# Two transformer blocks on one core: fewer key columns for the first token tile, and GpSimd scales the probabilities

## The reference, cut to what matters

```python
# sliding ("swa" in the kernel): chunks of 64 keys, this one and the two before it
mask = (k // 64 <= q // 64) & (k // 64 >= q // 64 - 2)
# forgetting ("fox"): blocks of 128 queries, keys up to the end of the block
s = jnp.einsum('bqhd,bkhd->bhqk', q[:, lo:hi], k[:, :hi]).astype(jnp.float32) * ATTN_SCALE
bias = cum[:, :, lo:hi, None] - cum[:, :, None, :hi]
s = jnp.where(causal, s + bias, NEG)
p = jax.nn.softmax(s, axis=-1).astype(v.dtype)
outs.append(jnp.einsum('bhqk,bkhd->bqhd', p, v[:, :hi]))
```

## Time and profile before

| | before |
|---|---|
| median of three runs | 2392.72 us (2390.62 to 2398.5) |
| span of the profiled execution | 2324.9 us |
| median less that span | 67.8 us |
| TensorE matmuls | 2118.6 us busy, 91% of the span |
| VectorE, ScalarE, GpSimd | 68%, 46%, 22% busy |
| DMA | 683 MB, mean 294 GB/s |

### The profile page before, as it was taken

The page is one execution under the profiler, slowest core; times in us unless marked ns, Lnnn a source line. Parts: engine busy times, 40 slices in busy tenths (PEclk is TensorE's granted clock), DMA queues, the critical chain, the costliest instruction groups (busy, mean ns, idle before and its releaser), DMA issues. The chain is left out here.

```text
span 2324.9 us, 27319 instructions
## 1 busy us (share of the span) xinstructions
PE 2118.6 (91%) x9328; PEld 1530.3 (66%) x9328; DVE 1575.4 (68%) x2602; ACT 1059.4 (46%) x1528; POOL 512.0 (22%) x550
## 2 busy tenths in 40 slices
PE   7999999877777777789999999999999999999996
PEld 6998867322222222247599887578888888888785
DVE  5775237666666666544555432578898998889986
ACT  3495014222222212113444324367777777777764
POOL 0000007777777777720000010000000000000000
PEclk9999999999999999999999999999999999999998
DMA  8544429999999999996254643279999999999993
GB/s 312 172 146 181 168 93 379 404 410 409 410 409 409 409 409 409 409 349 202 91 175 143 228 162 127 100 246 329 362 351 365 350 366 369 344 365 350 367 365 112
DMA packets 356584, 683.39 MB, mean 294 GB/s; under 512 B 14016, under 2 KB 222016, under 8 KB 356352
## 3 DMA queue, kind: packets, MB, share of 16 engines
q1 hardware_dynamic: 279008, 401.24, 50.8%
q0 software_dynamic: 77472, 280.80, 30.5%
HBM read 679.88 MB, written 2.10 MB: 293 GB/s over the span
## 5 line engine op out<-in xcount | busy, mean ns | idle before, releaser
L2264 DVE TENSOR_TENSOR weights_low<-weight_ring,piece_hi 128x2048 fp32r<-128x2048 f32 (+1 forms) x286 | 590.1, 2109 | 42.0 <-ACT piece_hi L1205 36.7
L1465 PE MATMUL psum<-weight_ring,region 128*128 128x512 f32 x988 | 478.2, 610 | 143.0 <-DMA weight_ring<-in_peer_v,region 141.5
L1205 ACT ACTIVATE piece_hi<-weight_ring 128x2048 fp32r<-128x2048 f32 (+1 forms) x286 | 494.7, 1768 | 30.4 <-PE psum L1694 27.8
L1465 PEld LDWEIGHTS psum<-weight_ring,region 128*128 128x128 f32 x988 | 169.2, 189 | 451.6 <-issue 303.0
L2083 DVE CUSTOM_DVE_ANT_0 weight_ring<-weight_ring,psum 128x1024 f32<-128x1024 f32 x224 | 273.6, 1222 | 206.8 <-DMA weight_ring<-in_peer_u,region 206.8
L1681 PE MATMUL psum<-piece_hi,tokens_hi 128*128 128x512 f32 x704 | 284.1, 404 | 2.4 <-DVE work_tok L2316 1.3
L841 POOL DMA_INDIRECT weight_ring<-in_peer_u,region x256 | 247.9, 968 | 140.7 <-DVE region L2057 53.0
L1683 PE MATMUL psum<-piece_hi,tokens_low 128*128 128x512 f32 x704 | 278.1, 395 | 0.0
L1682 PE MATMUL psum<-weights_low,tokens_hi 128*128 128x512 f32 x704 | 277.9, 395 | 0.0
L852 POOL DMA_INDIRECT weight_ring<-in_peer_v,region x256 | 242.3, 947 | 90.7 <-issue 70.3
L1053 ACT ACTIVATE region<-constants,region 128x128 f32<-128x128 f32 x247 | 88.4, 395 | 284.9 <-PE psum L1465 210.8
(11 more groups left out here) (317 smaller groups left out, 3428.7 us busy)
## 6 DMA issues: line engine op xcount, KB each, us to landing
weight_ring<-in_w_exp_in SPq DMA_DIRECT2D x176, 1024.0 KB, 11.8
weight_ring<-in_w_exp_out SPq DMA_DIRECT2D x48, 1536.0 KB, 10.0
weight_ring<-in_w_in SPq DMA_DIRECT2D x12, 2048.0 KB, 7.7
weight_ring<-in_w_ffn_in SPq DMA_DIRECT2D x22, 1024.0 KB, 7.7
weight_ring<-in_w_exp_out SPq DMA_DIRECT2D x8, 2048.0 KB, 8.6
weight_ring<-in_w_out SPq DMA_DIRECT2D x6, 2048.0 KB, 8.4
weight_ring<-in_w_in_fox SPq DMA_DIRECT2D x5, 2048.0 KB, 7.8
weight_ring<-in_w_ffn_out SPq DMA_DIRECT2D x6, 1536.0 KB, 6.6
```

The source lines that it names most:

```text
L1205: act.activation(dst, src, ACT.Copy).then_inc(e_hi, 1)
L1465: ins = pe.matmul(psum[:, peer_bank(t, half), :], diag[:, k, :], v_row(n)[:, 512 * half:512 * half + 512], start=(s < TILES and k == 0), s ...
L2264: dve.tensor_tensor(low_of(n), piece(n), hi_of(n).bitcast(F32), ALU.subtract).then_inc(e_low, 1)
```

## The change

1. For sliding and forgetting heads, tile 0 works on 128 keys (`keys_seen`): its score matmul, the maximum, the exponential and the scaling have 128 columns in place of 256. The transpose of block (key tile 1, token tile 0) is left out, so that three transposes are left and the copy out of PSUM has 384 columns. The second value matmul runs over the last 128 tokens alone. The sink of tile 0 stands in column 128.
2. In all 42 heads GpSimd scales both tiles' probabilities, one instruction for each tile, and counts both on one semaphore. ScalarE's L930 and VectorE's L1844 go, and TensorE waits for that one semaphore.
3. GpSimd's queue: the scalings of each stage are put between its DMAs. Of the norm rows, rows 4 and 5 come ahead of the scalings of att2[0], and the others behind them.

```diff
+CAUSAL = ("swa", "fox")
+def keys_seen(kind, t):
+    return (t + 1) * P if kind in CAUSAL else S
...
+    def turned_blocks(kind):
+        return [(k, t) for k in range(TILES) for t in range(TILES) if k * P < keys_seen(kind, t)]
+
+    def turned_keys(g, k):
+        blocks = turned_blocks(heads[g][0])
+        own_blocks = [i for i, (kk, _) in enumerate(blocks) if kk == k]
+        flat = pt_buf[g % 2].rearrange("p k s -> p (k s)")
+        return blocks[own_blocks[0]][1] * P, flat[:, own_blocks[0] * P:(own_blocks[-1] + 1) * P]
...
+        def probabilities(base, n):
+            for g in range(base, base + n):
+                b = g % 2
+                pool.wait_ge(sums_ready, g + 1)
+                for t in range(TILES):
+                    p = p_buf[b][:, t, 0:keys_seen(heads[g][0], t)]
+                    pool.tensor_scalar(p, p, den[:, 2 * b + t:2 * b + t + 1], None, ALU.mult).then_inc(probs_ready, 1)
+
         pool.wait_ge(product_ready, pl.nth["in", N_IN - 1])
         pool.dma_start(x_tok[:, :, :], a["x"][0].rearrange("(t p) n -> p t n", p=P)).then_inc(x_again, 16)
+        probabilities(pl.att1, N1)
         pool.wait_ge(merged, KD)
...
-        for i in range(4, late_row):
+        ROWS_AHEAD = 6
+        for i in range(4, ROWS_AHEAD):
+            load_row(i)
+        probabilities(pl.att2[0], SH + MH2)
+        for i in range(ROWS_AHEAD, late_row):
             load_row(i)
         pool.wait_ge(cum_ready, 1)
...
+        probabilities(pl.att2[1], SH + MH2)
         pool.wait_ge(normed, HALVES * TILES * 7)
...
-                    copy_out(("T", g), pt_buf[g % 2])
-                if 1 <= i <= n:
-                    g = base + i - 1
-                    b = g % 2
-                    act.wait_ge(sums_ready, g + 1)
-                    for t in range(TILES - 1):
-                        ins = act.activation(p_buf[b][:, t, 0:S], p_buf[b][:, t, 0:S], ACT.Copy, scale=den[:, 2 * b + t:2 * b + t + 1])
-                    ins.then_inc(probs_ready, 1)
+                    flat = pt_buf[g % 2].rearrange("p k s -> p (k s)")
+                    copy_out(("T", g), flat[:, 0:P * len(turned_blocks(heads[g][0]))])
...
-                    n_exp = S + 1 if kind in ("self1", "swa") else S
+                        n_exp = keys_seen(kind, t) + (kind in ("self1", "swa"))
...
+                seen = keys_seen(kind, t)
+                ins = pe.matmul(bank[:, t * S:t * S + seen], queries(kind, h)[:, t * P:(t + 1) * P], keys(kind, h)[:, 0:seen],
+                                start=True, stop=True)
...
-                    pe.wait_ge(probs_ready, g + 1)
-                    pe.wait_ge(last_probs_ready, g + 1)
+                    pe.wait_ge(probs_ready, TILES * (g + 1))
                     bank = begin(("T", g))
-                    for k in range(TILES):
-                        for t in range(TILES):
-                            ins = pe.transpose(bank[:, k * S + t * P:k * S + (t + 1) * P], p_buf[g % 2][:, t, k * P:(k + 1) * P], ident)
+                    for i_turned, (k, t) in enumerate(turned_blocks(heads[g][0])):
+                        ins = pe.transpose(bank[:, i_turned * P:(i_turned + 1) * P], p_buf[g % 2][:, t, k * P:(k + 1) * P], ident)
...
-                        ins = pe.matmul(bank[:, 0:S], values(*heads[g], k), pt_buf[g % 2][:, k, :], start=(k == 0), stop=(k == TILES - 1))
+                        first, turned = turned_keys(g, k)
+                        ins = pe.matmul(bank[:, first:S], values(*heads[g], k), turned, start=(k == 0), stop=(k == TILES - 1),
+                                        skip_group_check=True)
...
-            last = TILES - 1
-            dve.tensor_scalar(p_buf[b][:, last, 0:S], p_buf[b][:, last, 0:S], den[:, 2 * b + last:2 * b + last + 1], None, ALU.mult)\
-               .then_inc(last_probs_ready, 1)
...
-                        dve.tensor_copy(s_buf[b][:, :, S], sink.to_broadcast([P, TILES]))
+                        places = [t * (S + 1) + keys_seen(kind, t) for t in range(TILES)]
+                        flat = s_buf[b].rearrange("p t s -> p (t s)")
+                        dve.tensor_copy(flat[:, places[0]:places[1] + 1:places[1] - places[0]], sink.to_broadcast([P, TILES]))
                     for t in range(TILES):
-                        ins = dve.tensor_tensor_reduce(s_buf[b][:, t, 0:S], bank[:, t, :], C(mask)[:, t * S:(t + 1) * S] if mask else no_mask,
-                                                       scale, -3.0e38, ALU.add, ALU.max, m[:, t:t + 1])
+                        seen = keys_seen(kind, t)
+                        ins = dve.tensor_tensor_reduce(s_buf[b][:, t, 0:seen], bank[:, t, 0:seen],
+                                                       C(mask)[:, t * S:t * S + seen] if mask else no_mask, scale, -3.0e38, ALU.add, ALU.max, m[:, t:t + 1])
```

More of the change, by code:

```diff
@@ L597, in two_blocks @@
     max_ready, exp_ready, probs_ready = sem("max_ready"), sem("exp_ready"), sem("probs_ready")
-    sums_ready, last_probs_ready = sem("sums_ready"), sem("last_probs_ready")
+    sums_ready = sem("sums_ready")
     lam_exp, lam_ready, conv_ready = sem("lam_exp"), sem("lam_ready"), sem("conv_ready")
@@ L1326, in score @@
             for t in range(TILES):
-                ins = pe.matmul(bank[:, t * S:(t + 1) * S], queries(kind, h)[:, t * P:(t + 1) * P], keys(kind, h), start=True, stop=True)
+                seen = keys_seen(kind, t)
+                ins = pe.matmul(bank[:, t * S:t * S + seen], queries(kind, h)[:, t * P:(t + 1) * P], keys(kind, h)[:, 0:seen],
+                                start=True, stop=True)
             end(ins, ("S", g))
```

## The result

The changed kernel takes 2409.2 us (median, 2404.8 to 2410.9), the kernel before 2391.7 in the same comparison. The ratio is 1.0059 with an interval of 1.0046 to 1.0073: slower by 11 to 17 us (the two medians lie 17.5 apart), where 5.8 faster was forecast and 2398 was the end of the range.

A forecast was written before the change was run, and what follows sets the result against it. TensorE was taken to bound the attention stages, the other engines' path just hidden. Heads -2.6, -4.0, +1.0, +0.5, openings +0.35, -0.4 and ends -0.6 summed to -5.8 us: 2386.9 against 2392.7, range 2380 to 2398.

The forecast's parts named there:

- what a scaling on GpSimd costs: Attention heads: no row showed it; taken as 0.43 us for 256 columns and 0.28 for 128, between 0.101 and 0.968.
- x: Time of one GpSimd scaling of 256 columns, taken as 0.43 us, the middle of VectorE's 0.355 and ScalarE's 0.508.
- rival 2: Attention steps: GpSimd is slow and its two scalings in series become the bound; +7.0 us at 0.71, +19 at 0.968; chance 0.24.
- The rule that spoke against the change: The skill keeps elementwise work on VectorE, about twice as fast; by twice VectorE's price the sum is about +7 us.
- step = (W+L)/2: Attention step when path L, scores issued to turning, exceeds TensorE's work W; 1.825 to 2.325 us against 2.16 before.
- The sum: Whole kernel: changes of all heads, openings and ends add to -5.8 us; in x, 45.8x - 25.5, zero at 0.56.
- The narrow records: Sliding and forgetting heads: a 128-column record costs 0.124 us against 0.216, so a step's TensorE work falls to 1.68.
- Rival 3: Narrow matmuls stay dear because the weight load sets their pace; -1.4 us, 2391.3; chance 0.06.
- The other engines: ScalarE and VectorE in attention: 1 to 4 us of 22 to spare, more after the change, so costed at nothing.
- The openings: Stage starts: att1's first scaling takes 0.86 us in place of 0.51, +0.35; att2's two openings save 0.22 each, -0.4.
- The clock, which I left out: att1's opening: TensorE's clock is already at half after an idle of 2.9 us; nothing more was counted for it.
- The end: Three stage ends: the last turning comes 1.3 us after the one before, in place of 1.86; together -0.6 us.

The follow-up runs named there:

- e8: Changed kernel with GpSimd's scaling written as a product of the tile and its broadcast column: 2325.1 us against 2326.4 for the kernel before.
- e5: Changed kernel with three buffers of probabilities and one more step between exponentials and turning: 2383.7 us against 2393.2 for the kernel before.
- e4: Changed kernel run again without an edit: 2406.5 us against 2393.2 for the kernel before.
- e2: Changed kernel with no head narrowed, GpSimd scaling both tiles of 256 keys: 2348.2 us against 2325.8 for the kernel before.
- e1: Changed kernel with only the narrow tile, scaling left on ScalarE and VectorE: 2318.2 us against 2325.8 for the kernel before.
- e6: Kernel before with several forms of GpSimd instruction added and each waited for; the scaling of 256 columns took 0.923 us.
- e7: Changed kernel with the extra step of e5, but scaled by ScalarE and VectorE as in e1: ratio 0.9967 to the kernel before.
- e9: Changed kernel with the edits of both e5 and e8: 2309.7 us against 2326.4 for the kernel before, ratio 0.9931.
- e0: Kernel before, run and profiled again without an edit: median 2326.4 us.

## Why the prediction was wrong

**The step that failed** is "what a scaling on GpSimd costs". I named its bounds, 0.101 and 0.968, and took x = 0.43 by the nearest rows, those of two other engines. It measured 0.92. That is beyond the 0.71 from which rival 2, two scalings in series as the bound, is slower than a measurement's 0.3%, and rival 2 is what happened. I gave it 0.24, and 0.12 to the part beyond 0.71: rows of another engine are no rows of this one, and should have weighed little between ends so far apart. The rule that spoke against the change had the right sign. The Trainium skill (GPSIMD Engine Reference, "Performance versus the Vector engine" and "Engine selection") has GpSimd about twice as slow as VectorE for operations with two inputs. The scaling, one tile and a column of scalars, takes 0.92 here against 0.355, 2.6 times; no run has VectorE's time for two inputs. The Trainium skill (GPSIMD Engine Reference, "Engine selection") calls GpSimd with one input roughly line-rate, from which I had estimated 0.32. The scaling is far from that, and the copy, at 0.40, is nearest to it.

**The mechanism held**, with the measured price in the forecast's own formula, step = (W+L)/2:

| heads | forecast, x = 0.43 | formula, x = 0.92 and 0.60 | measured |
|---|---|---|---|
| sliding | 1.945 | 2.35 | 2.38 |
| forgetting | 1.825 | 2.23 | 2.26 |
| windowed | 2.325 | 2.82 | 2.79 |
| memory: path L, from S to T | 2.25 | 3.23 | 3.27 |

The forgetting heads' 2.26 is from 1518.48 to 1523.00, the windowed heads' 2.79 from 216.91 to 228.05 in four steps. e8 is the formula's test at another price (2.10 worked out, 2.11 measured), and e5 takes the path out of the step altogether.

**The sum** by the formula is 45.8 x 0.92 - 25.5 = +16.6 us, and the stages have +12.4 (e4) and +11.6 (first trace). Part of the difference can be read in att2[0] of the two first traces. I counted a step for each of its 16 heads, but only twelve, from T(1) to T(13), are steps of the formula (1159.77 to 1189.18, before 1088.93 to 1115.12: +3.22). The last two turnings cost +1.32. The opening up to T(1) is 1.33 shorter, where I had put 0.22, because its scores are narrower too and nothing there waits for a scaling. The same excess shows in e2 (+27 expected, +22.4 measured). It touches the size of the forecast, not its sign. The rest of the difference is not resolved.

**The narrow records** cost what the earlier trace rows said: V 0.65 and S 0.66, W 1.64 in e5 against 1.68. Rival 3 is out. **The other engines**, near full before and costed at nothing after the change, did not bind in the changed kernel. They decide e1, where both scalings stay: the gain of the narrow tile alone stops at VectorE.

**The openings.** In att1 T(0) comes 4.47 us after the score matmuls of the second head end (206.37 to 210.84), and came 3.06 after them before: +1.4, where 0.35 was forecast, by the same price. The clock, which I left out, adds to it in one of two traces. Three stretches of 3 us of the changed kernel's first trace, with the granted clock third from the right, and below them two of e4, the same kernel:

```profile
207.00:210.00 3.00, 0.00 (x0) 0.00 (x0) 0.42 (x3) 2.56 (x9) 1.06 (x2) 1.00 0.97 282
210.00:213.00 3.00, 2.16 (x7) 1.92 (x8) 1.27 (x6) 1.00 (x4) 2.59 (x3) 0.58 1.05 418
213.00:216.00 3.00, 3.00 (x14) 2.23 (x12) 1.57 (x8) 2.20 (x8) 0.96 (x2) 0.85 1.03 403
```

```profile
209.00:212.00 3.00, 2.80 (x9) 2.34 (x10) 0.62 (x5) 1.58 (x5) 1.94 (x3) 0.50 1.04 419
212.00:215.00 3.00, 3.00 (x11) 2.55 (x10) 1.52 (x8) 1.57 (x5) 1.61 (x2) 0.50 1.04 398
```

In the first trace the clock is back at 1.00 from 214 on, no later than before (0.50 from 210 to 213). In e4 it is at half until 215, and its att1 is 0.9 us longer (38.36 against 37.48). So some 0.9 of e4's 12.4 us is clock and not path.

**The end and the place of the cost.** The last turning of att1 comes 1.80 after the one before it (1.86 before), not the 1.3 forecast: GpSimd is still at its two scalings, as rival 2 had it for 0.968. Outside the attention no loss shows, as I had it: 11.1 us separate the spans of e4 and e6 (the kernel before with a few GpSimd instructions more), the stages 12.4.

## What to carry to other kernels

Here work moved to an idle engine was free only where the path had room for that engine's latency. Find the wait that ends the path, write the step as (work + path)/2 or whatever the order of the queue makes of it, and see at which price the sign turns; where the trace has no row of that operation on that engine, the price must be measured before anything else, in a stretch where nothing depends on it, and in several forms. If the engine is fast enough in throughput but not in latency, one more buffer and one more step of distance can turn the same loss into a gain (from +13 to -10 us here by the ratios, and -16 with the cheaper form), as long as another engine is not the next bound (e7).

## What the runs showed of the hardware that was not expected

- On GpSimd a scaling by a column, float32, 128x256, takes 0.92 us, the same product with the column broadcast as a second input 0.61, a product of two full tiles 0.72, a copy 0.40. VectorE takes 0.355 for the scaling, ScalarE 0.508.
- GpSimd's times were the same beside a busy VectorE as beside an idle one (0.924 in the changed kernel and 0.923 in e6; 0.614 in e8 and 0.612 in e6). VectorE's long instructions there read PSUM; other mixes were not tried.
- During or right after TensorE's idle in att1's opening its granted clock fell to half, 1.2 GHz, in ten of twelve traces (idle of 2.0 to 4.3 us; 0.50 to 0.62 in the stretch from 209 or 210 on), but not in e5 and e9, which sat idle for 3.45 and 2.76 us. In e9, the same columns as above:

```profile
208.00:211.00 3.00, 0.62 (x5) 0.62 (x6) 1.19 (x7) 1.79 (x8) 1.85 (x4) 1.00 0.98 375
211.00:214.00 3.00, 2.09 (x13) 1.65 (x12) 2.64 (x14) 2.47 (x10) 1.51 (x3) 1.00 1.03 415
```

The length of the idle alone does not decide it; what does was not tried. It is probably most of why att1, which has no narrowed head, is 1.8 us shorter in e9 than before: in e0 TensorE is fully busy at 0.50 from 208 to 211, and at full clock that work would take 1.5 us less (an estimate from these rows).
